# A gated linear attention layer in a two-layer trunk: gate chain beside the input projection, chunk states apart from the products, outputs summed chunk by chunk

## The chip, the core and the metric

One core of one Trainium2 chip runs the whole program. The metric is the device time of one launch in microseconds (us), the median of several runs. The engines are PE (TensorE, matrix products), DVE (VectorE), ACT (ScalarE), POOL (GpSimd) and SP (SyncE, which issues the weight loads). All data is fp32.

## The reference, cut to what matters

There are 512 tokens (256 context, 256 latent) and two layers. Each layer is FFN, token mixing, FFN. The change is in the token mixing of the second layer: a chunked gated linear attention (GLA) with 4 heads (key width 128, value width 256), both directions, chunks of 64 tokens, latent output alone.

```python
logs = [(jax.nn.log_sigmoid((gd @ g_up[d] + g_b[d]).astype(f32)) / GLA_NORMALIZER) for d, gd in ...]
# one direction
b = jnp.cumsum(g, axis=3)                      # within each chunk
scores = einsum(q * jnp.exp(b - b_ref), k * jnp.exp(b_ref - b))
o_intra = einsum(jnp.where(lower, scores, 0.0), v)
q_in = q * jnp.exp(b); k_out = k * jnp.exp(b_last - b); d_last = jnp.exp(b_last[:, :, :, 0])
def step(S, inp):
    o = jnp.einsum('bhck,bhkv->bhcv', qc, S)
    S = S * dc[..., None] + jnp.einsum('bhck,bhcv->bhkv', kc, vc)
    return S, o
# readout
y = o * lax.rsqrt(jnp.mean(jnp.square(o), -1, keepdims=True) + GLA_EPS) * norm_g
return y.reshape(B, T, GLA_DV) * jax.nn.silu(og.astype(jnp.float32))   # then @ w_out
```

## The kernel before

The program is written engine by engine: each engine has its own list of instructions, and semaphores (`S("name")`, `wait_ge`, `then_inc`) tie the lists together. An engine runs its list in order, so a wait holds all that stands behind it. Six sublayers run one after the other; sublayer 4 is the GLA, and its part is `odd_mixer()` in each list, followed by `norm()`.

**Projection.** `OD_TILES` (L2255) lists 33 tiles: 4 of k, one of the low-rank gate input (gd), 4 of q, 16 of v, 8 of the output gate (og). Weights come in pieces of 128x1024. SP loads them into two slots in `arena[:, 0:8192]`, ACT rounds each to `w_hi` (helper `hi`, L642), POOL forms the remainder `w_lo` (L2141), and PE makes three products of every pair. Four pieces are held at a time (columns 8192 to 16384 of the arena). Tile i goes to PSUM bank i mod 8 and ACT copies it out (`z1_done`). The inputs `u_hi` and `u_lo` hold columns 16384 to 24576.

**Gate chain.** Behind the last tile PE makes 8 products of the gate input (32 rows, 512 columns) with `gup`; ACT takes their absolute value, then Exp and Ln over all 4096 columns (L892, L894); DVE takes the minimum with 0 (L2019), subtracts (L2023), sums along the tokens (scan, L2028) and forms the exponents; ACT takes the exponentials (L897 to L906); DVE multiplies them into the keys and queries (L2053 to L2060). The chain's buffers lie where `u_hi` and the weight pieces were.

**Chunks.** PE transposes the keys (L1455, L1461), makes the state products of the context and the scores, then in three rounds the products of the keys and values of one chunk in each direction. In each round DVE adds the old state and multiplies by the decay (L2093, L2096), and the next round waits for that (`gst`). The states `gst` lie in the two weight slots. With all four states there, PE makes the outputs: for each of 8 value tiles, the 128-column product with the masked scores and four 64-column products of states and queries per pair of chunks.

**Readout.** DVE copies the outputs (L2104), ACT squares (L916), PE sums with `ones`, ACT takes Ln and Exp of the sums (L921, L926), DVE multiplies with weight, root and gate (L2113, L2117). ACT and DVE split the result (`out_hi` L734, `out_lo` L1651) and PE starts `project_out`. SP waits for the outputs (`go_mm`) before it loads the output weights; ACT splits their first four pieces behind the Exp.

## Time and profile before

| | us |
|---|---|
| median of 3 runs (2499.55 to 2501.19) | 2499.87 |
| the profiled execution | 2498.56 |
| its span in the profile | 2496.8 |
| projection of the GLA, PE from 1982 to 2083 | 101 |
| from there to the start of `project_out` | 155 |
| PE busy in these 155 us | 84.3 |

### The profile page before, as it was taken

To read this page: it belongs to the slowest core of one execution; us is meant where nothing else is said; L and a number is where in the kernel's file an instruction comes from. 1 tells how busy PE (TensorE), PEld (TensorE's weight loads), DVE (VectorE), ACT (ScalarE), POOL (GpSimd) and SP (SyncE) were. 2 spreads that over 40 slices of the span, in tenths; PEclk is the share of its full clock that TensorE was granted. 3 is DMA by queue.
4 is the path that set the end of the run, shared out by engine and by line. 5 is a ranking of instruction groups with operands and counts; after the bars stand their busy time and mean duration, and the time that the engine had idled before them with its cause. 6 is when DMAs were issued, how large, how long until landed. Compare 5 with 4: busy or idle time off the path is not lost.

```text
span 2496.8 us, 35562 instructions
## 1 busy us (share of the span) xinstructions
PE 2232.4 (89%) x15487; PEld 1800.6 (72%) x15487; DVE 929.5 (37%) x1352; ACT 741.1 (30%) x1065; POOL 937.4 (38%) x429
## 2 busy tenths in 40 slices
PE   5999999799946999978999999899999795578996
PEld 2678877588435888846778777577888594578996
DVE  3322222532487455545330332532131503536213
ACT  2422221533131122135221222522122534126433
POOL 0334434343042121023444334434444352026884
PEclk9999999899977898879999999899999897659998
DMA  9463353230000000022543453263332130023551
GB/s 329 134 227 123 98 193 135 85 134 27 9 0 2 2 3 7 3 101 76 192 171 127 143 203 110 93 212 109 101 101 85 62 121 1 0 101 104 200 170 67
DMA packets 176090, 259.66 MB, mean 104 GB/s; under 512 B 3925, under 2 KB 146275, under 8 KB 175876
## 3 DMA queue, kind: packets, MB, share of 16 engines
q1 hardware_dynamic: 173338, 252.65, 29.9%
q10 hardware_dynamic: 2602, 4.78, 0.5%
q8 instruction: 122, 2.00, 0.3%
q14 instruction: 28, 0.23, 0.0%
HBM read 256.37 MB, written 1.05 MB: 103 GB/s over the span
## 4 chain that ended last, share of the span: by engine, by line
PE 82%; DVE 10%; ACT 5%; issue 1%; DMA 1%; ACTq 0%; SPq 0%; POOL 0%; DVEq 0%; POOLq 0%
PE psum L959 81%; ACT arena L670 1%; ACT u_hi L675 1%; DVE h L1697 1%; DMA arena<-in_ada_w 1%; DVE arena L1854 1%; DVE arena L1865 1%; DMA arena<-in_x 1%; DVE tmp L1710 0%; ACT tmp L720 0%; DVE arena L1831 0%; ACTq L583 0%; DVE arena L2028 0%; PE psum L1301 0%; ACT L730 0%
## 5 line engine op out<-in xcount | busy, mean ns | idle before, releaser
L2141 POOL TENSOR_TENSOR w_lo<-arena,w_hi 128x1024 fp32r<-128x1024 f32 x332 | 811.7, 2450 | 1164.1 <-ACT w_hi L642 1161.8
L959 PE MATMUL psum<-u_hi,w_hi 128*128 128x512 f32 (+1 forms) x1888 | 698.7, 370 | 73.4 <-ACT u_hi L675 39.5
L959 PE MATMUL psum<-u_hi,w_lo 128*128 128x512 f32 (+1 forms) x1888 | 688.1, 365 | 0.0
L959 PE MATMUL psum<-u_lo,w_hi 128*128 128x512 f32 (+1 forms) x1888 | 669.2, 362 | 0.0
L642 ACT ACTIVATE w_hi<-arena 128x1024 fp32r<-128x1024 f32 x332 | 348.4, 1055 | 745.2 <-PE psum L959 733.1
L959 PEld LDWEIGHTS psum<-u_hi,w_hi 128*128 128x128 f32 x1888 | 361.9, 192 | 171.3 <-issue 41.0
L959 PE MATMUL psum<-arena 64*64 64x64 f32 (+8 forms) x5892 | 420.1, 267 | 53.8 <-DVE arena L1887 18.4
L959 PEld LDWEIGHTS psum<-arena 64*64 64x64 f32 (+5 forms) x5892 | 327.4, 158 | 141.0 <-issue 75.3
L959 PEld LDWEIGHTS psum<-u_hi,w_lo 128*128 128x128 f32 x1888 | 362.4, 192 | 54.3
L959 PEld LDWEIGHTS psum<-u_lo,w_hi 128*128 128x128 f32 x1888 | 357.7, 190 | 52.6 <-issue 0.2
L1667 DVE TENSOR_TENSOR tmp<-psum,tmp 128x512 f32<-128x512 f32 (+1 forms) x88 | 54.9, 624 | 592.4 <-ACT tmp L694 592.4
L959 PE MATMUL psum<-hid_hi,w_hi 128*128 128x512 f32 (+1 forms) x704 | 257.4, 366 | 1.7 <-POOL w_lo L2141 1.1
L959 PE MATMUL psum<-hid_hi,w_lo 128*128 128x512 f32 (+1 forms) x704 | 255.3, 363 | 0.0
L959 PE MATMUL psum<-hid_lo,w_hi 128*128 128x512 f32 (+1 forms) x704 | 255.2, 363 | 0.0
L1671 DVE TENSOR_TENSOR hid_lo<-tmp,hid_hi 128x512 f32 (+1 forms) x88 | 200.8, 2282 | 10.8
L959 PEld LDWEIGHTS psum<-hid_hi,w_hi 128*128 128x128 f32 x704 | 132.9, 189 | 24.3 <-DVE mods L1605 1.7
L959 PEld LDWEIGHTS psum<-hid_lo,w_hi 128*128 128x128 f32 x704 | 132.9, 189 | 21.1 <-issue 0.7
L959 PEld LDWEIGHTS psum<-hid_hi,w_lo 128*128 128x128 f32 x704 | 132.9, 189 | 20.8
L694 ACT ACTIVATE tmp<-psum 128x512 f32<-128x512 f32 (+1 forms) x88 | 47.9, 544 | 303.1 <-PE psum L959 303.1
L819 ACT ACTIVATE arena<-psum 128x256 f32<-128x256 f32 x96 | 35.7, 386 | 210.5 <-PE psum L959 208.3
L1681 DVE SCALAR_TENSOR_TENSOR h<-psum,mods,h 128x256 f32<-128x256 f32 x56 | 22.3, 476 | 197.2 <-PE psum L959 197.2
L1697 DVE SCALAR_TENSOR_TENSOR h<-psum,mods,h 128x256 f32<-128x256 f32 x80 | 35.2, 478 | 147.8 <-PE psum L959 147.8
(248 smaller groups left out, 1596.1 us busy)
## 6 DMA issues: line engine op xcount, KB each, us to landing
arena<-in_ada_w SPq DMA_DIRECT2D x48, 1536.0 KB, 6.8
arena<-in_ffn_wg SPq DMA_DIRECT2D x44, 1024.0 KB, 5.3
arena<-in_ffn_wu SPq DMA_DIRECT2D x44, 1024.0 KB, 7.9
arena<-in_ffn_wd SPq DMA_DIRECT2D x20, 2048.0 KB, 8.4
arena<-in_ev_w_in SPq DMA_DIRECT2D x6, 2048.0 KB, 7.7
arena<-in_od_w_in SPq DMA_DIRECT2D x6, 2048.0 KB, 8.4
arena<-in_ffn_wd SPq DMA_DIRECT2D x4, 1024.0 KB, 4.8
arena<-in_ev_w_out SPq DMA_DIRECT2D x2, 2048.0 KB, 10.4
```

The costliest lines, as they stand in the source:

```text
L642: act.activation(piece_shape(split_hi(pc), src), src, ACT.Copy).then_inc(S("hi_done"), 1)
L670: ins = act.activation(us[:, k, s_], hs[:, k, s_], ACT.Identity, scale=modv[:, 24 * (g % 3) + 8 + k, s_:s_ + 1], bias=modv[:, 24 * (g % 3) ...
L675: act.activation(uhv[:, k, T0:NT], uv[:, k, T0:NT], ACT.Copy).then_inc(S("u_hi"), 1)
L694: act.activation(tmp[:, jf * NT:jf * NT + TN], bank[2 * jf][:, 0:TN], ACT.Silu)\
L819: act.activation(blocks(zs[:, d].rearrange("p h t -> p (h t)"), m, d), blocks(bank[d], m, d), ACT.Copy).then_inc(S("zs"), 1)
L959: return pe.matmul(dst, w, x, start=first_, stop=last, skip_group_check=True)
L1667: ve.tensor_tensor(prod, bank[2 * jf + 1][:, 0:TN], prod, ALU.mult).then_inc(S("pairs_free"), 1)
L1671: ve.tensor_tensor(hid_lo[:, at], prod, hid_hi[:, at].bitcast(F32), ALU.subtract)\
L1697: ins = ve.scalar_tensor_tensor(out=hs[:, k, s], in0=bank[b][:, lo:lo + SEG], scalar=modv[:, 24 * (g % 3) + 16 + k, s:s + 1], in1=hs[:, k, s],
L1854: ve.tensor_scalar(dst, tile_of(aa[d], c), col("k_a", c), small[:, 20 + c:21 + c], ALU.mult, ALU.add).then_inc(S("ve_steps"), v.step())
L1865: ve.reciprocal(prep2, prep2).then_inc(S("ve_steps"), v.step())
L2141: pool.tensor_tensor(piece_shape(split_lo(pc), src), src, piece_shape(split_hi(pc).bitcast(F32), src), ALU.subtract).then_inc(S("lo_done"), 1)
```

## The change

It does four things. The 8 gate products become tiles of `OD_TILES` (kind "lg", no weight piece), two behind each q tile; DVE takes the minimum from PSUM, ACT the absolute value, and Exp, Ln and the exponentials run per direction between the copies of tiles (`LG_EXP`, `LG_LN`, `LG_FACTORS` say behind which). DVE forms all keys, queries and decay pairs, then raises `lat_in`. The buffers of the chain move to columns that are free during the projection, and the states to the home of `u_hi` and `u_lo`, so the weight slots stay free: SP loads the output weights without a wait, and POOL and ACT may split them early. The key transposes are one series of 32. The chunk products no longer wait for the states: ACT copies them to SBUF times the decay, and DVE adds old state times decay in one instruction (24 of 256 columns). The outputs are summed in passes: the 128-column products for all 8 tiles, then four passes of 64-column products, one for each state index, into banks 4 to 7. In the readout ACT squares from PSUM, DVE multiplies PSUM with the gate (already times the norm weight), and the Ln table is loaded ahead.

```diff
@@ -350,20 +350,25 @@
...
-        gcs = arena[:, 16384:20480].rearrange("p (d c t) -> p d c t", d=2, c=4)
+        lga = [big[:, 9728:11776], big[:, 11776:13824]]
+        lgb = [arena[:, 24576:26624], arena[:, 41984:44032]]
...
-        gst = arena[:, 0:8192].rearrange("p (d n c v) -> p d n c v", d=2, n=4, c=4)
...
+        gst = arena[:, 16384:24576].rearrange("p (d n c v) -> p d n c v", d=2, n=4, c=4)
...
@@ -563,7 +568,6 @@
...
-                    sp.wait_ge(S("go_mm"), 4)
                     load_cols("odd_out", g, A["od_w_out"][0], [(0, 512), (512, 512)])
...
@@ -875,6 +879,9 @@
...
+                    elif kind == "lg":
+                        act.wait_ge(S("lg_min"), j + 1)
+                        ins = act.activation(gcs[j // 4][:, j % 4], bank[i % 8], ACT.Abs, bias=col("gla_b", j))
...
@@ -883,38 +890,42 @@
...
-                    act.wait_ge(S("lg_psum"), q + 1)
-                    act.activation(gcs[:, d, c], bank[q], ACT.Abs, bias=col("gla_b", q)).then_inc(S("lg_abs"), 1)
...
-                act.activation(arena[:, 16384:20480], arena[:, 16384:20480], ACT.Exp, scale=-1.0).then_inc(S("lg_exp"), 1)
-                act.wait_ge(S("lg_exp"), 1)
-                act.activation(arena[:, 16384:20480], arena[:, 16384:20480], ACT.Ln, bias=eps[:, 3:4]).then_inc(S("lg_ln"), 1)
...
+                    for d, at in enumerate(LG_EXP):
+                        if (kind, j) == at:
+                            act.wait_ge(S("z1_done"), i + 1)
+                            act.activation(lga[d], lga[d], ACT.Exp, scale=-1.0).then_inc(S("lg_exp"), 1)
+                    for d, at in enumerate(LG_LN):
+                        if (kind, j) == at:
+                            act.wait_ge(S("lg_exp"), d + 1)
+                            act.activation(lga[d], lga[d], ACT.Ln, bias=eps[:, 3:4]).then_inc(S("lg_ln"), 1)
+                    for d, at in enumerate(LG_FACTORS):
...
+                            act.wait_ge(S("lat_arg"), d + 1)
+                            act.activation(fl(kout[d]), fl(kout[d]), ACT.Exp, scale=1 / GLA_N)
...
+                            act.activation(fl(qh[d]), fl(kh[d]), ACT.Exp, scale=sign / GLA_N)
+                            act.activation(fl(kh[d]), fl(kh[d]), ACT.Exp, scale=-sign / GLA_N).then_inc(S("lat_exp"), 1)
...
+                for n, q in enumerate(TURNS):
+                    act.wait_ge(S("ko_turned"), n + 1)
+                    dst = kot[n // 2][:, n % 2] if n < 4 else kht[(n - 4) // 2][:, n % 2]
+                    act.activation(dst, bank[q], ACT.Copy).then_inc(S("kot"), 1)
+                for n in range(3):
+                    act.wait_ge(S("gs_mm"), n + 2)
+                    for c in range(4):
+                        for d in range(2):
+                            act.activation(gst[:, d, n + 1, c], bank[4 * (n % 2) + 2 * d + c // 2]
+                                           [:, (c % 2) * HV:(c % 2 + 1) * HV], ACT.Identity,
+                                           scale=gpair[:, d, c, n:n + 1]).then_inc(S("gkv"), 1)
+                for q in range(PIECES):
+                    hi("odd_out", 4, q)
+                act.activation(small[:, 16:17], eps[:, 3:4], ACT.Ln)
...
+                for c in range(4):
+                    act.wait_ge(S("go_mm"), c + 1)
+                    act.activation(sq2[:, 2 * c:2 * c + 2].rearrange("p c t -> p (c t)"), bank[4 + c], ACT.Square)\
...
@@ -1423,10 +1432,17 @@
...
+                    if kind == "lg":
+                        if j == 0:
+                            pe.wait_ge(S("z1_done"), 5)
+                            pe.wait_ge(S("ld_gla"), 48)
+                        mm(bank[i % 8], gup[:, j // 4, (j % 4) * P:(j % 4 + 1) * P], ggd, True, True)\
+                            .then_inc(S("z1_psum"), 1)
+                        continue
...
@@ -1443,69 +1459,65 @@
...
-                pe.wait_ge(S("z1_done"), len(OD_TILES))
-                pe.wait_ge(S("ld_gla"), 48)
-                for q in range(8):
-                    mm(bank[q], gup[:, q // 4, (q % 4) * P:(q % 4 + 1) * P], ggd, True, True)\
-                        .then_inc(S("lg_psum"), 1)
...
+                pe.wait_ge(S("lat_in"), 1)
+                for n, q in enumerate(TURNS):
+                    pe.wait_ge(S("z1_done"), len(OD_TILES) - 7 + n)
...
+                for d in (1, 0):
+                    pe.wait_ge(S("kot"), 8 if d == 0 else 4)
...
-                    pe.wait_ge(S("gst"), n + 1)
...
+                    if n == 0:
+                        pe.wait_ge(S("gst"), 2)
+                    elif n == 1:
+                        pe.wait_ge(S("pm"), 4)
+                    else:
+                        pe.wait_ge(S("gkv"), 8)
+                    for c in range(4):
+                        for d in range(2):
+                            ch = XCHUNK(d, n)
+                            lo = 64 * (ch % 2)
+                            ins = mm(bank[4 * (n % 2) + 2 * d + c // 2][:, (c % 2) * HV:(c % 2 + 1) * HV],
+                                     kht[d][lo:lo + 64, ch // 2, c * P:(c + 1) * P],
                                      gvt[lo:lo + 64, 2 + ch // 2, c * HV:(c + 1) * HV], True, True)
-                    ins.then_inc(S("gs_mm"), 1)
...
+                pe.wait_ge(S("gkv"), 16)
...
+                        mm(out_of(vt_)[:, b * P:(b + 1) * P], gvt[:, 2 + b, vt_ * P:(vt_ + 1) * P],
+                           pm[:, 0, b, vt_ // 2], vt_ % 2 == 0 and b == 0, False)
+                for n in range(4):
+                    for vt_ in range(8):
+                        c = vt_ // 2
+                        if n and vt_ % 2 == 0:
+                            pe.wait_ge(S("gst"), 2 + 8 * (n - 1) + 2 * (c + 1))
+                        for d in range(2):
+                            ch = XCHUNK(d, n)
+                            ins = mm(out_of(vt_)[:, 64 * ch:64 * ch + 64], gst[:, d, n, c, (vt_ % 2) * P:(vt_ % 2 + 1) * P],
+                                     qh[d][:, c, 64 * ch:64 * ch + 64], False, n == 3)
+                        if n == 3 and vt_ % 2:
+                            ins.then_inc(S("go_mm"), 1)
...
@@ -2012,70 +2024,66 @@
...
-                ve.wait_ge(S("z1_done"), len(OD_TILES))
...
+                for i, (q, kind, j) in enumerate(OD_TILES):
+                    if kind == "lg":
+                        ve.wait_ge(S("z1_psum"), i + 1)
+                        ve.tensor_scalar(gg[j // 4][:, j % 4], bank[i % 8], col("gla_b", j), 0.0, ALU.add, ALU.min)\
+                            .then_inc(S("lg_min"), 1)
...
+                    ve.tensor_tensor(lgb[d], lgb[d], lga[d], ALU.subtract).then_inc(S("ve_steps"), v.step())
...
+                        ve.tensor_tensor_scan(gcs[d][:, c], greset, gg[d][:, c], 0.0, ALU.mult, ALU.add)\
...
+                    ve.sem_inc(S("lat_arg"), 1)
+                ve.wait_ge(S("z1_done"), OD_TILES.index((8, "q", 3)) + 1)
...
+                    ve.wait_ge(S("lat_exp"), d + 1)
+                    ve.tensor_tensor(kout[d], kout[d], gk[:, :, 0:SEG], ALU.mult).then_inc(S("ve_steps"), v.step())
+                    ve.tensor_tensor(kh[d], gk[:, :, SEG:NT], kh[d], ALU.mult).then_inc(S("ve_steps"), v.step())
+                    ve.scalar_tensor_tensor(out=qh[d], in0=gq, scalar=HK ** -0.5, in1=qh[d],
...
+                ve.sem_inc(S("lat_in"), 1)
...
@@ -2085,36 +2093,24 @@
...
-                        ve.tensor_tensor(nxt, psum[:, b0 + 2 * d:b0 + 2 * d + 2, :]
-                                               .rearrange("p b (c v) -> p (b c) v", c=2), gst[:, d, n], ALU.add).then_inc(S("ve_steps"), v.step())
-                        ve.wait_ge(S("ve_steps"), v.n)
-                        ins = ve.tensor_tensor(nxt, nxt, gpair[:, d, :, n].unsqueeze(2).to_broadcast([P, 4, HV]),
...
+                    for c in range(4):
+                        ve.wait_ge(S("gst"), 2 if n == 0 else 2 + 8 * (n - 1) + 2 * (c + 1))
+                        for d in range(2):
+                            ve.wait_ge(S("gkv"), 8 * n + 2 * c + d + 1)
+                            ve.scalar_tensor_tensor(out=gst[:, d, n + 1, c], in0=gst[:, d, n, c], scalar=gpair[:, d, c, n:n + 1],
+                                                    in1=gst[:, d, n + 1, c], op0=ALU.mult, op1=ALU.add)\
+                                .then_inc(S("gst"), 1)
...
+                    ve.tensor_tensor(pair_(go), bank[4 + c], pair_(gog), ALU.mult).then_inc(S("ve_steps"), v.step())
...
+                    ve.tensor_tensor(o, o, grs[:, 2 * i:2 * i + 2].unsqueeze(2).to_broadcast([P, 2, 2, SEG]), ALU.mult)\
+                        .then_inc(S("mixed"), 1)
...
@@ -2240,8 +2236,8 @@
...
-                    pool.wait_ge(S("z1_done"), len(OD_TILES))
-                    pool.memset(big[:, 11776:13824], 0.0).then_inc(S("pm_zero"), 1)
+                    pool.wait_ge(S("lat_arg"), 2)
+                    pool.memset(lga[1], 0.0).then_inc(S("pm_zero"), 1)
...
@@ -2252,8 +2248,11 @@
...
-OD_TILES = ([(j, "k", j) for j in range(4)] + [(4, "gd", 0)] + [(5 + j, "q", j) for j in range(4)]
+OD_TILES = ([(j, "k", j) for j in range(4)] + [(4, "gd", 0)]
+            + [at for j in range(4) for at in ((5 + j, "q", j), (None, "lg", 2 * j), (None, "lg", 2 * j + 1))]
             + [(9 + 2 * (j // 4), "v", j) for j in range(16)] + [(17 + j, "og", j) for j in range(8)])
+LG_EXP, LG_LN = (("lg", 3), ("lg", 7)), (("q", 2), ("v", 0))
+LG_FACTORS = (("v", 7), ("v", 15))
```

On PE behind the last projection tile, before: 32 products make the context states and the scores, 24 the chunks, and the outputs go tile by tile. Each row is one run of equal instructions.

```order
L1455 MATMUL psum<-ident,arena 128x128 x16
L1461 MATMUL psum<-ident,arena 128x128 x16
L959 MATMUL psum<-arena 128x256 x16
L959 MATMUL psum<-arena 128x128 x16
L959 MATMUL psum<-arena 128x256 x24
L959 MATMUL psum<-arena 128x128
L959 MATMUL psum<-arena 128x64 x4
L959 MATMUL psum<-arena 128x128
```

The same place after:

```order
L1467 MATMUL psum<-ident,arena 128x128 x32
L968 MATMUL psum<-arena 128x256 x16
L968 MATMUL psum<-arena 128x128 x16
L968 MATMUL psum<-arena 128x256 x24
L968 MATMUL psum<-arena 128x128 x16
L968 MATMUL psum<-arena 128x64 x64
L968 MATMUL psum<-arena,ones 128x256 x8
```

The counts are the same; all 128-column output products now stand ahead of all 64-column ones.

On ACT between the last q tiles and the v tiles of the projection, after (L886 and L888 copy q and v tiles, L884 takes the absolute value, L896 Exp and L900 Ln of one direction):

```order
L884 ACTIVATE arena<-psum,par 128x512 x2
L896 ACTIVATE arena<-arena 128x2048
L646 ACTIVATE w_hi<-arena 128x1024
L886 ACTIVATE arena<-psum 128x256
L900 ACT_TABLE_LOAD
L900 ACTIVATE arena<-arena,eps 128x2048
L884 ACTIVATE arena<-psum,par 128x512 x2
L646 ACTIVATE w_hi<-arena 128x1024
L886 ACTIVATE arena<-psum 128x256
L884 ACTIVATE arena<-psum,par 128x512 x2
L896 ACT_TABLE_LOAD
L896 ACTIVATE arena<-arena 128x2048
```

Before, only `hi` (L642) and the copies (L879, L881) stand here, and this is what stood behind the whole projection:

```order
L890 ACTIVATE arena<-psum,par 128x512 x8
L892 ACT_TABLE_LOAD
L892 ACTIVATE arena<-arena 128x4096
L894 ACT_TABLE_LOAD
L894 ACTIVATE arena<-arena,eps 128x4096
```

Exp and Ln moved in front of the copies of the v tiles and of the splitting of their weights.

## Rows read from the trace of the kernel before

**Rows 1.** The page's chain that ended last, by engine.

```profile
PE 82%; DVE 10%; ACT 5%; issue 1%; DMA 1%; ACTq 0%; SPq 0%; POOL 0%; DVEq 0%; POOLq 0%
```

**Rows 2.** Windows: start:end, length, busy us by engine, PEclk, DMA.

```profile
1982.00:2083.00 101.00, 100.83 (x762) 97.15 (x760) 0.00 (x0) 41.05 (x64) 55.75 (x24) 1.00 0.31 108
2083.00:2238.00 155.00, 84.27 (x337) 70.49 (x337) 71.57 (x76) 40.50 (x47) 12.94 (x5) 0.59 0.08 28
```

**Rows 3.** Timeline of PE: start, us, instruction, idle before and releaser.

```profile
2083.31 11.29 PE L959 MATMUL psum<-arena 32*128 32x512 f32 x16 [0.47 <-ACT arena L884]
2128.97 3.67 PE L1455 MATMUL psum<-ident,arena 128*128 128x128 f32 x16 [34.37 <-DVEq L2055]
2135.24 3.67 PE L1461 MATMUL psum<-ident,arena 128*128 128x128 f32 x16 [2.59 <-DVEq L2062]
2138.71 11.64 PE L959 MATMUL psum<-arena 128*128 128x256 f32 x64
2151.75 2.96 PE L959 MATMUL psum<-arena 64*128 64x256 f32 x16 [1.41 <-DVE arena L2082]
2159.69 5.65 PE L959 MATMUL psum<-arena 64*128 64x256 f32 x16 [4.97 <-DVE arena L2096]
...
2181.05 34.40 PE L959 MATMUL psum<-arena 128*128 128x128 f32 x160 [5.03 <-DVE arena L2096]
2215.24 5.65 PE L959 MATMUL psum<-arena,ones 128*128 128x256 f32 x16
2237.91 0.55 PE L959 MATMUL psum<-u_hi,w_hi 128*128 128x256 f32 x1 [17.02 <-DVE u_lo L1651]
```

**Rows 4.** Windows around the clock's changes, columns as in Rows 2.

```profile
2086.00:2087.00 1.00, 1.00 (x3) 0.48 (x2) 0.86 (x3) 0.70 (x2) 0.00 (x0) 0.55 0.00 0
...
2141.00:2143.00 2.00, 2.00 (x11) 1.76 (x10) 0.00 (x0) 0.00 (x0) 0.00 (x0) 1.00 0.00 0
2147.00:2149.00 2.00, 2.00 (x20) 2.00 (x20) 2.00 (x2) 0.00 (x0) 0.00 (x0) 1.00 0.00 0
...
2185.00:2190.00 5.00, 5.00 (x25) 5.00 (x25) 0.05 (x1) 0.00 (x0) 0.00 (x0) 0.50 0.02 3
...
2242.00:2243.00 1.00, 1.00 (x7) 1.00 (x7) 0.00 (x0) 0.00 (x0) 0.00 (x0) 0.50 1.11 351
```

**Rows 5.** Timeline of ACT, columns as in Rows 3.

```profile
1979.26 1.08 ACT L670 ACTIVATE arena<-h,mods 128x256 f32<-128x256 f32 x2
...
2080.00 0.38 ACT L884 ACTIVATE arena<-psum 128x256 f32<-128x256 f32 x1 [2.50 <-PE psum L959]
...
2121.35 1.91 ACT L897 ACTIVATE arena<-arena 128x2048 f32<-128x2048 f32 x1 [14.78 <-DVEq L2037]
...
2130.37 1.21 ACT L909 ACTIVATE arena<-psum 128x512 f32<-128x512 f32 x2
...
2221.63 1.28 ACT L926 ACT_TABLE_LOAD   x1
2222.92 1.15 ACT L926 ACTIVATE arena<-arena 128x512 f32<-128x512 f32 x2
```

**Rows 6.** Timeline of POOL, columns as in Rows 3.

```profile
2225.09 11.13 POOL L2141 TENSOR_TENSOR w_lo<-arena,w_hi 128x1024 fp32r<-128x1024 f32 x4 [139.97 <-ACT w_hi L642]
```

**Rows 7.** Timeline of DVE, columns as in Rows 3.

```profile
2105.37 4.42 DVE L2023 TENSOR_TENSOR arena<-arena 128x4096 f32<-128x4096 f32 x1 [9.26 <-ACT arena L894]
2109.83 9.03 DVE L2028 TENSOR_TENSOR_SCAN arena<-arena 128x512 f32<-128x512 f32 x8
...
2146.89 2.35 DVE L2074 TENSOR_TENSOR arena<-psum,small 128x1024 f32<-128x1024 f32 x2 [11.07 <-PE psum L959]
...
2234.06 3.24 DVE L2117 TENSOR_TENSOR arena<-arena 128x1024 f32<-128x1024 f32 x1
```

**Rows 8.** Window in the first layer, columns as in Rows 2.

```profile
1069.00:1070.00 1.00, 0.69 (x4) 0.50 (x3) 0.00 (x0) 0.27 (x1) 0.00 (x0) 0.50 0.00 0
```

**Rows 9.** Groups by form in the 4 us before it (1065 to 1069): busy, mean ns.

```profile
L959 PE MATMUL psum<-arena 128*128 128x64 f32 x14 | 2.5, 295 | 0.0
L959 PE MATMUL psum<-arena 64*128 64x64 f32 x16 | 1.8, 296 | 0.0
```

204 lines of the change are left out of this document (66 added, 138 removed).

## The prediction, made before the changed kernel ran

> **What bounds the kernel now.** The page's chain by engine comes first: PE carries 82% of the chain, DVE 10%, ACT 5% [rows 1]. So a change off PE pays only where PE waits for it or runs at the low clock. The windows by stage come next [rows 2]. In the projection PE is busy for 100.83 of 101 us at clock 1.00. In the 155 us behind it PE is busy for 84.27 us, at a mean of 0.59, and no other engine for more than 71.6. This stretch is a chain of engines handing over, and PE's share runs mostly at half speed. The timeline of PE names the pieces [rows 3]: 11.3 us of gate products, 34.4 us of waiting for the gate chain on ACT and DVE, transposes, 11.6 us of state and score products, three rounds of chunk products with 5 us of DVE behind each, 34.4 us of output products, 5.7 us of sums and 17.0 us of waiting for the readout. The change touches all of it and nothing else, so I sum the new path from the end of the projection's products (2083.31 less 0.47 idle: 2082.84) to the first product of project_out (2237.91): 155.1 us before.
>
> **Gate products in the projection.** Before, 8 products took 11.29 us, the first 2.8 us at full clock until it fell at 2086 [rows 3, 4], the rest at half. With p for one at full clock, 2.8/p + 8.4/2p = 8 gives p = 0.87. Eight between the q tiles add 6.9 us to PE, which has no idle time there to hide them. The bound above is 14 (all at half), below 6.8. I take full clock: between pairs of them (1.7 us) stands a dense tile of 2.9 us (0.38 + 2.50 between the copies of two tiles [rows 5]).
>
> **The gate chain behind them.** The wait of 34.4 us and one of 2.6 go [rows 3], if the chain is over before PE's last tile. What is new beside the projection is ACT work: 8 absolute values, two Exp and two Ln of 2048 columns (1.91 each), five table loads of 1.28 [rows 5]. The tight place is the second direction's exponentials behind tile v15: ACT splits two pieces (2.0), copies (0.4), does three exponentials of 1024 columns (half of 1.91 and a little, 3.4 in all), then splits the piece for tile og4 (1.1), and POOL needs 2.4 to 2.8 (11.13 for four [rows 6]). That is 9.3 to 9.7 us, and og4 starts 4 tiles of 2.88, or 11.5 us, behind v15: no stall, with 1.8 us to spare. DVE's part: 4.4 for the subtractions, 9.0 for the scans [rows 7], some 6 for exponents, all while 16 v tiles (46 us) run; then 3.6 us of products per direction. The last are done some 10 us behind v15, 13 us before the projection ends. So lat_in costs nothing; each microsecond beyond those 13 would cost one. The projection ends 6.9 us later and nothing else.
>
> **Transposes and context states**, from that end as zero. Two series of 3.67 us at half clock become one of 32; straight behind dense tiles I take full clock, 3.7 us. ACT's eight copies (0.6 each, 1.21 for two [rows 5]) end near 5; the first state products need four of them, the others eight, at 7.2, so nothing waits. State and score products took 11.64 us, of which 2.2 at half clock until 2141 [rows 3, 4]: 10.5 at full. End: 14.2.
>
> **Chunk products.** A round took 2.96 at full clock and 5.65 at half [rows 3]. The first needs DVE's first states (2.35 [rows 7], done at 13) and runs 14.2 to 17.2; the second runs to 20.2. The third needs ACT's 8 copies of the first: one of 256 columns lies between 0.38 (plain) and 0.54 (two with scale and bias in 1.08) [rows 5]; with scale alone I take 0.45, 3.6 in all, from 17.3 to 20.9. The third ends at 24.0, ACT's second set at 24.5, and with it banks 4 to 7 are free. Heads now alternate between the two halves of the rows, which could shorten a round to no less than 1.5; I keep 3.0, the row's own, as ACT sets two of the three steps. DVE's 24 additions follow ACT and end near 29, before the passes need them. The path from the first round to the last state was 30 us.
>
> **Outputs.** 80 products give 160 records in 34.40 us, 0.215 each at half clock, 0.107 at full (20 in 2.0 us at clock 1.00 [rows 4]); 64 columns cost as much as 128. The 128-column ones: 32 records, 3.4 us, to 28.0. The passes are 128 records. Here the clock decides. For 34 us of such products before it never rose [rows 3, 4], and in the first layer it had fallen to 0.50 [rows 8] behind a stretch made up mostly of 64-column products [rows 9]. I let it fall 4 us into the passes: 37 records at full, 91 at 0.215, 23.6 us in all, to 51.6. Bounds: 13.7 (never falls) and 27.5.
>
> **Readout.** The sums need their 5.65 us [rows 3], the squares beside them: 57.2. Then Ln (0.7), the Exp table (1.28) and the first Exp (0.6) [rows 5]: 60.0 with handovers. Before, the DVE step behind was slowed while POOL split four pieces (3.24 us for 1024 columns [rows 7], 11.13 on POOL [rows 6]). Now the output weights are there early, ACT splits them at 29 to 33 and POOL is done near 42. Two products of 1.2 (half of 2.35 [rows 7]) end at 62.4, and PE starts at 63.0. The copy out of PSUM and a multiplication are gone; the multiplication by the norm weight (1 to 2.5 us on DVE) lies beside the transposes. If POOL were not done, the old 3.24 would return, 4 us in all.
>
> The Trainium skill has a rule on this: ScalarE: Activation LUTs, "Table sets: the hidden batching unit", says one set has both exp and ln, so a change from one to the other needs no load. By it the readout would be 1.3 us shorter. The trace differs: the load of 1.28 stands between Ln and Exp [rows 5], and the sum keeps it.
>
> **Sum.** 6.9 + 63.0 = 69.9 against 155.1: 85.2 us less. The span goes from 2496.8 to 2411.6, the profiled execution from 2498.56 to 2413.4, and the median, which stood 1.3 above it, to 2414.7. Behind the start of project_out nothing changes: PE starts it at half clock, as before.
>
> **Rivals.** (1) The clock holds through the passes. For it: PE no longer pauses for more than a microsecond there. Against: [rows 8, 9]. Passes 13.7 instead of 23.6, sums 3.4 instead of 5.65: 12.1 less, 2402.6. (2) It falls already in the chunk products, which use 64 rows. For it: it fell during products of 32 rows [rows 3, 4]. Against: in 2.96 us of them it held [rows 3]. Second and third round at 5.65 (+4.5, as part hides behind ACT), the 128-column products +3.4, the start of the passes +4.0: 11.9 more, 2426.6. (3) It falls in the transposes: 3.7 us of them stand in one series, and it comes back 2.2 to 5 us into the products (2.2 at 2138.71; at 2242 it was still low, 4 us after 2237.91 [rows 3, 4]). Half of that and up to 1.8 us of the transposes is lost, 1.1 to 4.3: 2417.5. The Trainium skill, TensorE: Matmul & The Clock Gate, "Part 4: PE-mode transpose", says that transposes do not engage the full clock; the trace speaks against it, as the rise 2.2 us behind a series of transposes came sooner than the one without. (4) ACT or POOL late in the projection by more than the 1.8 us: up to 6 us of stalls at og4 to og7, 2418. (5) The chain is not hidden: lat_in comes behind the projection. DVE would have to take more than twice its 20 us; with 5 us over the end, 2420. (6) Slower: the gate products bring the clock down in the projection and it stays at half to its end. The 27 tiles behind them (77.8 us) and the products (6.9) would double, +84.7, and with (2) the time is 2511. It decides from 85 us of such work, so only if it never comes back; the products of project_out, the same as these, brought it back some 5 us after 2237.91 at clock 0.50 [rows 4]. A brief fall costs 2 to 5 us and lies in (4).
>
> **How the numbers follow.** Forecast 0.52, (1) 0.12, (2) 0.15, (3) 0.10, (4) 0.08, (5) 0.02, (6) 0.01. The forecast's own bounds are the moment of the fall (4 us either way), the rounds (2 less) and ACT's copies (1.5 either way). The range from 2401 to 2426 takes these, (1), (3), (4), and half of (2). About 0.2% (5 us) can be told from no change; all but (6) lie far beyond that: faster 0.98, within 0.01, slower 0.01.
>
> **What would show it.** Projection of 108 us at clock 1.00 with no PE idle: the first two parts. PE's first transpose within 0.5 us of the last tile: chain hidden. Third chunk round waiting under 1 us for ACT: the rounds. Granted clock in the 64-column passes: forecast against (1) and (2); clock in the transposes: (3). From the last pass to project_out 11 us against 22.5. A wait for w_lo in the og tiles would be (4).

## The result and the profile of the changed kernel

The changed kernel takes 2395.78 us (median of 4 runs, 2389.39 to 2404.31) against 2499.71 for the kernel before: a ratio of 0.960, 95% interval 0.957 to 0.963. The forecast was 2414.7 with a range from 2401 to 2426, so the kernel is faster than the range allows. Its profiled execution has a span of 2387.6 us, 109.2 less than before.

The chain that ended last, by engine, answers to [rows 1]; PE's share grew from 82% as the waits for DVE and ACT went:

```profile
PE 84%; DVE 8%; ACT 5%; issue 1%; DMA 1%; ACTq 0%; SPq 0%; POOL 0%; DVEq 0%; POOLq 0%
```

Windows of the changed kernel (start:end, length, busy us by engine, PEclk, DMA), to be held against [rows 2]: most of the projection, the stretch behind it up to the first product of project_out, and the first microseconds of that.

```profile
1970.00:2079.00 109.00, 109.00 (x775) 99.89 (x774) 52.09 (x38) 64.61 (x88) 64.32 (x25) 1.00 0.37 126
2080.00:2130.00 50.00, 41.82 (x323) 38.92 (x322) 23.59 (x44) 27.12 (x56) 9.58 (x4) 0.96 0.19 62
2130.00:2135.00 5.00, 5.00 (x32) 5.00 (x32) 1.90 (x6) 1.00 (x2) 0.00 (x0) 0.71 0.00 0
```

PE's timeline of the changed kernel, to be held against [rows 3]. The row at 2083.18 holds the state and score products and two chunk rounds in one piece, that at 2098.90 the last round, that at 2101.92 all output products, and that at 2119.80 the sums.

```profile
1958.15 0.80 PE L968 MATMUL psum<-u_hi,w_hi 128*128 128x512 f32 x1 [6.05 <-ACT u_hi L679]
...
2079.68 3.66 PE L1467 MATMUL psum<-ident,arena 128*128 128x128 f32 x32
...
2083.18 14.30 PE L968 MATMUL psum<-arena 128*128 128x256 f32 x96
2098.90 2.00 PE L968 MATMUL psum<-arena 64*128 64x256 f32 x16 [1.43 <-ACT arena L919]
2101.92 18.05 PE L968 MATMUL psum<-arena 128*128 128x128 f32 x160 [1.02 <-ACT arena L919]
...
2119.80 3.67 PE L968 MATMUL psum<-arena,ones 128*128 128x256 f32 x16
2129.21 0.55 PE L968 MATMUL psum<-u_hi,w_hi 128*128 128x256 f32 x1 [5.74 <-DVE u_lo L1663]
```

Between 2079.68 and 2129.21 lie 49.5 us; before it was 155.1. PE waits 8.2 of them (1.4, 1.0 and 5.7), and the granted clock is 1.00 up to the readout's wait. The same place in the kernel before: the first product of this projection stands at 1969.53, so that the projection took 113.3 us; now it is 121.5.

The other engines, to be held against [rows 5, 6, 7]. First ACT: its copies of the chunk products, its split of the output weights and the table load ahead of the readout's Exp. Then DVE: one of the key products beside the last og tiles, the pair products (the decay pairs), and its last step of the readout. Last POOL, which forms remainders of weights beside those key and pair products.

```profile
2095.82 8.88 ACT L919 ACTIVATE arena<-psum,small 128x256 f32<-128x256 f32 x24 [11.48 <-PE psum L968]
2104.40 4.08 ACT L646 ACTIVATE w_hi<-arena 128x1024 fp32r<-128x1024 f32 x4
...
2124.22 1.28 ACT L937 ACT_TABLE_LOAD   x1
```

```profile
2063.86 3.43 DVE L2066 TENSOR_TENSOR arena<-arena 128x1024 f32<-128x1024 f32 x1
...
2070.56 4.96 DVE L2071 TENSOR_TENSOR small<-small 128x4 f32<-128x4 f32 x6
...
2126.24 2.36 DVE L2112 TENSOR_TENSOR arena<-arena 128x1024 f32<-128x1024 f32 x2 [4.92 <-ACT arena L937]
```

```profile
2063.17 12.10 POOL L2137 TENSOR_TENSOR w_lo<-arena,w_hi 128x1024 fp32r<-128x1024 f32 x4 [0.31 <-ACT w_hi L646]
```

**Where the 109.2 us of the profiled pair came from.** The stretch behind the projection: 155.1 less 49.5, less the 8.2 that the projection grew: 97.3. Behind the start of project_out: 258.9 before (2496.8 less 2237.91), 258.4 now: 0.5. Ahead of the projection, in code that is the same in both: 11.4 (1969.53 less 1958.15). So two questions are left: why this part gave 12 us more than the 85.2 of my sum, and what the 11.4 us are.

### The profile page after: what moved, and what is told of

Its sections match the earlier page's. It is cut to its first block, busy times and chain, and to the rows that moved or that the text cites. A ratio compares the mean times of both kernels' runs of the same rounds, so it can differ in the third digit from the quotient of the medians.

```text
span 2387.6 us, 35611 instructions
## 1 busy us (share of the span) xinstructions
PE 2186.0 (92%) x15487; PEld 1764.1 (74%) x15487; DVE 929.5 (39%) x1354; ACT 750.6 (31%) x1097; POOL 942.9 (39%) x429
## 4 chain that ended last, share of the span: by engine, by line
PE 84%; DVE 8%; ACT 5%; issue 1%; DMA 1%; ACTq 0%; SPq 0%; POOL 0%; DVEq 0%; POOLq 0%
PE psum L968 83%; ACT arena L674 1%; ACT u_hi L679 1%; DVE h L1709 1%; DMA arena<-in_ada_w 1%; DVE arena L1866 1%; DVE arena L1877 1%; DMA arena<-in_x 1%; DVE tmp L1722 0%; ACT tmp L724 0%; ACTq L587 0%; DVE arena L1843 0%; PE psum L1310 0%; ACT L734 0%; DVE arena L2017 0%
## 5 line engine op out<-in xcount | busy, mean ns | idle before, releaser
L968 PE MATMUL psum<-arena 64*64 64x64 f32 (+8 forms) x5892 | 380.1, 258 | 39.4 <-DVE arena L1899 18.4
L968 PEld LDWEIGHTS psum<-arena 64*64 64x64 f32 (+5 forms) x5892 | 294.7, 150 | 117.7 <-issue 70.8
```

The lines of the kernel that those rows point to most:

```text
L968: return pe.matmul(dst, w, x, start=first_, stop=last, skip_group_check=True)
```

## The experiments

A stage time is that from the first transpose (or, where gate products stand ahead of it, from the end of the projection) to the first product of project_out; it is 49.5 in the changed kernel and repeats within 0.1 us. Products of 128 columns are called wide and those of 64 columns narrow; a filler is a product of the identity that nothing uses. The readings rest on the stage times and the timelines. The medians also hold what happens ahead of the stage, which differs by up to 20 us from execution to execution (last section of the experiments). Four kernels ran only once (e5_tiles_warm, e6_wide_last, e7_long_passes, e9_rounds_by_half), so nothing is read from their times.

### Pause and order: the tile order and the wait

The passes undone alone (e1_tiles), and the wait alone that this brings with it (e2_wait):

```diff
 # both
+                pe.wait_ge(S("gst"), 26)
 # e1_tiles alone
                 for vt_ in range(8):
+                    c, dst = vt_ // 2, out_of(vt_)
                     for b in range(2):
...
-                for n in range(4):
-                    for vt_ in range(8):
...
+                        mm(dst[:, b * P:(b + 1) * P], gvt[:, 2 + b, vt_ * P:(vt_ + 1) * P], pm[:, 0, b, c], True, False)
+                        for ch in (2 * b, 2 * b + 1):
+                            for d in range(2):
+                                ins = mm(dst[:, 64 * ch:64 * ch + 64],
+                                         gst[:, d, ch if d == 0 else 3 - ch, c, (vt_ % 2) * P:(vt_ % 2 + 1) * P],
+                                         qh[d][:, c, 64 * ch:64 * ch + 64], False, ch % 2 == 1 and d == 1)
...
```

> The changed kernel with its output products in the order of before: tile by tile, behind a wait for the last state. PE then pauses for some 5.4 us ahead of them (2100.9 to DVE's last addition at 2106.2 in the changed kernel's trace), as before it paused 5 us in each chunk round. Theory A (what decides is whether the clock is up when these products begin, and a pause of 5 us brings it down; they hold a full clock but do not raise it): the granted clock falls at the start of the outputs and stays at half, the 160 records take 34 us instead of 18, and the time is 4.4 + 16 to 19 us above the changed kernel, about 2417. Theory B (the order decides, passes hold the clock and tiles do not): the same numbers here, told apart by the next kernel. Theory C (neither matters, such products always run at full clock once the work ahead of them is dense on average): 18 us at clock 1.00, time 2400 or a little less.

> The changed kernel with one wait more: PE waits for the last state ahead of the 128-column output products, and the passes stay. Theory A (the pause brings the clock down, and the 64-column products do not bring it back): half clock through all outputs, 34 us, time about 2417, like the kernel with tiles. Theory B (the order by passes holds the clock): full clock, outputs 17 to 18 us, time 2400, and only the kernel with tiles is slow. Theory C: 2400 too, and both alike.

PE's timeline of e1_tiles (the output products, then the sums) and windows of it, then PE's output products in e2_wait and windows of that:

```profile
2125.72 34.37 PE L968 MATMUL psum<-arena 128*128 128x128 f32 x160 [5.40 <-DVE arena L2097]
...
2159.88 4.89 PE L968 MATMUL psum<-arena,ones 128*128 128x256 f32 x16
```

```profile
2124.00:2126.00 2.00, 0.28 (x1) 0.31 (x2) 1.57 (x4) 2.00 (x4) 0.87 (x1) 0.70 0.00 0
...
2156.00:2160.00 4.00, 4.00 (x21) 4.00 (x21) 0.00 (x0) 0.00 (x0) 0.00 (x0) 0.50 0.01 4
```

```profile
2116.73 20.88 PE L968 MATMUL psum<-arena 128*128 128x128 f32 x160 [5.41 <-DVE arena L2101]
```

```profile
2116.00:2122.00 6.00, 5.27 (x25) 5.30 (x26) 0.58 (x2) 4.36 (x6) 5.88 (x3) 0.50 0.01 3
2123.00:2124.00 1.00, 1.00 (x12) 1.00 (x11) 0.00 (x0) 0.00 (x0) 1.00 (x2) 1.00 0.00 0
```

Both pause 5.4 us and both start at half clock; the pause brings it down. But in e2_wait it is back 6 us later, while the 32 records of 128 columns run, and the narrow passes behind them run at full clock. In e1_tiles it stays low for all 34 us and comes back only in the sums (4.89 us, where the changed kernel has 3.67). The stages are 71.4 and 56.7 us, which is 21.9 and 7.2 more than in the changed kernel; the medians, 2425.81 and 2409.07 us, lie 30.0 and 13.3 above its 2395.8, so part of that is not the stage's. Theory A is right for the clock of one and wrong for the other (it had 2417 for both), B is wrong on the first step of e2_wait. What differs is where the wide products stand, or the order itself; and whether the tile order also brings a full clock down was not asked.

### Which products hold the clock, and which bring it back

Tile order without the pause (e5_tiles_warm), pause with the wide products behind the passes (e6_wide_last), and ten times the first pass (e7_long_passes):

```diff
 # e5_tiles_warm: e1_tiles with
-                pe.wait_ge(S("gst"), 26)
+                pe.wait_ge(S("gst"), 10)
-                                         gst[:, d, ch if d == 0 else 3 - ch, c, (vt_ % 2) * P:(vt_ % 2 + 1) * P],
+                                         gst[:, d, min(ch if d == 0 else 3 - ch, 1), c, (vt_ % 2) * P:(vt_ % 2 + 1) * P],
 # e6_wide_last: e2_wait with the loop of pm products moved behind the passes
 # e7_long_passes
-                for n in range(4):
+                for n in (0, 0, 0, 0, 0, 0, 0, 0, 0, 0, 1, 2, 3):
```

> Outputs tile by tile as in the kernel e1_tiles, but without the pause ahead of them: the products of the third and fourth chunk states read the second's, which are there (this leaves out the last two states' share of the outputs, not one product). What e1_tiles and e2_wait left open is whether the tile order only fails to bring a fallen clock back, or also brings a full one down. Theory B1 (it holds what it finds; only a pause brings the clock down): 160 records in 17 to 18 us at clock 1.00. Theory B2 (one wide product in five is too little work: the clock falls some microseconds into the tiles even without a pause): 34 us less what runs ahead of the fall, 28 to 31 us, and the pause in e1_tiles was not needed for its loss.

> The kernel e2_wait (a pause of 5.4 us, then the passes) with the 32 records of 128 columns behind the 128 records of 64 columns and not ahead of them. In e2_wait the clock came back 6 us into the outputs, when the wide ones were nearly through. Theory P (the row of wide products brings it back, the narrow ones of the passes would not): the passes run at half clock, 27.5 us, and the clock rises in the wide ones or behind them, 32 to 34 us in all. Theory Q (any unbroken row of products brings it back, and the tile order of e1_tiles failed for another reason): full clock after some 6 us, 20 to 21 us in all as in e2_wait.

> The changed kernel with its first pass done ten times and not once: 416 records of 64 columns behind the wide ones and not 128 (so its output products hold the first chunk's states ten times over). It asks how long such products hold a full clock that they find. In the changed kernel they held it for 13.7 us. Theory H (they hold it as long as PE does not pause): 44.6 us at clock 1.00. Theory F (the clock falls at some point of a long row of them, as it does in the first layer's stretch of such products): the fall shows in the granted clock and the passes take 50 to 85 us; where it falls says how near the changed kernel is to it.

PE's output products in e5_tiles_warm, in e6_wide_last and in e7_long_passes (each row runs over wide and narrow products alike), and windows of the last two:

```profile
2108.12 18.05 PE L968 MATMUL psum<-arena 128*128 128x128 f32 x160 [0.97 <-issue]
```

```profile
2105.88 32.41 PE L968 MATMUL psum<-arena 128*128 128x64 f32 x160 [5.40 <-DVE arena L2102]
```

```profile
2107.00:2133.00 26.00, 26.00 (x124) 26.00 (x123) 0.00 (x0) 2.51 (x4) 7.88 (x4) 0.50 0.26 81
2133.00:2136.00 3.00, 3.00 (x16) 3.00 (x17) 0.11 (x1) 0.60 (x1) 0.00 (x0) 0.52 0.00 0
2136.00:2138.00 2.00, 2.00 (x20) 2.00 (x19) 1.28 (x2) 1.17 (x2) 0.00 (x0) 1.00 0.03 8
```

```profile
2110.29 50.21 PE L968 MATMUL psum<-arena 128*128 128x128 f32 x448 [1.02 <-ACT arena L919]
```

```profile
2114.00:2160.00 46.00, 46.00 (x414) 46.00 (x414) 1.85 (x4) 5.89 (x9) 9.58 (x4) 1.00 0.15 47
```

Without the pause the tile order runs as fast as the passes (18.05 us, the changed kernel's own figure): B1, not B2. In e6_wide_last PE is busy for 26 us without a break at 0.50, and the clock rises only when the wide products run, some 30 us behind the pause: P, not Q. Time alone did not raise it, as in e1_tiles it was still low after 34 us. And the clock stayed full through 46 us of narrow products: H. So for this stage the order by passes gives nothing to the clock by itself. It gives two other things: PE can begin before the last state is there, so the 5.4 us pause is gone, and where a pause does happen, the wide products stand in one piece and bring the clock back.

The Trainium skill, TensorE: Matmul & The Clock Gate, "Why this matters for your kernels", has continuous work as what brings the full clock and idle gaps as what loses it. The traces agree on the gap (0.50 behind 5.4 us in three kernels) and differ on the work: 26 us of unbroken products of 64 columns stayed at 0.50.

### The same with nothing of the change in it

The kernel before with 22 products of the identity ahead of the second and third round and of the outputs:

```diff
+                    for _ in range(22 if n else 0):
+                        mm(bank[4 * ((n + 1) % 2)][:, 0:P], ident[:, :], ident[:, :], True, True)
                     pe.wait_ge(S("gst"), n + 1)
...
+                for _ in range(22):
+                    mm(bank[0][:, 0:P], ident[:, :], ident[:, :], True, True)
                 pe.wait_ge(S("gst"), 4)
```

> The kernel before, with one thing added: while PE waits 5 us for DVE ahead of the second and third chunk round and ahead of the outputs, it runs 22 products of 128 columns of the identity (22 x 0.215 = 4.7 us at full clock) into a bank that is free. Nothing of the change is in it. If pauses bring the clock down, wide products keep it up and narrow ones hold it, the rounds take 2.96 us and not 5.65, the output products in their old tile order 18 and not 34.4, the sums 3.67 and not 5.65: 2.7 + 2.7 + 16.4 + 2.0 = 24 us less than the kernel before. Rival (the tile order itself is slow, or DVE's steps suffer from PE's writes): less than 10 us.

```profile
2151.83 5.18 PE L959 MATMUL psum<-ident 128*128 128x128 f32 x44
2156.94 2.96 PE L959 MATMUL psum<-arena 64*128 64x256 f32 x16
...
2172.93 18.08 PE L959 MATMUL psum<-arena 128*128 128x128 f32 x160
2190.84 4.03 PE L959 MATMUL psum<-arena,ones 128*128 128x256 f32 x16
...
2211.76 0.55 PE L959 MATMUL psum<-u_hi,w_hi 128*128 128x256 f32 x1 [16.89 <-DVE u_lo L1655]
```

The rounds take 2.96 us each, the outputs 18.08 where [rows 3] had 34.40, the stage 131.7 instead of 155.1: 23.3 us less, forecast 24. The ratio to the kernel before is 0.988 (0.985 to 0.992), a median of 2467.38 us. The interval is clear of 1. So some 23 us of what the change gained could be had by fillers in three pauses, without any of its other parts.

### The other parts, one at a time

The gates and their chain behind the projection; the output weights late; a round direction by direction:

```diff
 # e3_gates_behind: the eight "lg" tiles at the end of OD_TILES, and
+LG_EXP, LG_LN = (("lg", 3), ("lg", 7)), (("lg", 7), ("lg", 7))
+LG_FACTORS = (("lg", 7), ("lg", 7))
 # e4_late_weights: hi("odd_out", 4, q) behind the last Exp again, and
+                    sp.wait_ge(S("go_mm"), 4)
                     load_cols("odd_out", g, A["od_w_out"][0], [(0, 512), (512, 512)])
 # e9_rounds_by_half
-                    for c in range(4):
-                        for d in range(2):
+                    for d in range(2):
+                        for c in range(4):
```

> The changed kernel with the first part undone: the eight gate products and the whole chain of exponents stand behind the projection, everything after them as changed. The chain by the durations of the changed kernel's trace: products 6.9, minimum and absolute value 1.5, Exp 1.9, table 1.3, Ln 2.0, DVE 9.6 for one direction and 10.8 for the other, ACT exponentials 3.2, DVE products and pairs 5 to 8: some 43 us from the last tile, 36 more than in the changed kernel. Theory A: the transposes begin at half clock and the clock comes back in the state and score products as it did before (3.7 + 2 to 5 us lost), and from there the rounds and passes follow without a pause and hold it: outputs 18 us at clock 1.00, time about 2396 + 41 = 2437. Rival D (the clock in the passes was held by the dense work of the projection shortly before and not by the products themselves): outputs at half clock, 34 us, time about 2454. If the chain costs less than 30 us more, the sizes in this sum are wrong.

> The changed kernel with the output weights loaded and split late, as before: the load waits for the last output product, ACT splits behind the exponentials. POOL's four pieces then lie beside the readout. My prediction's step: DVE's two products go from 1.2 to up to 3.2 us each and PE's project_out waits 4 us longer, or more if the load itself (2 MB or so) and the splits are late: from the last output product to project_out before took 22.5 us, in the changed kernel it takes 12. Theory A (the late weights are what made the rest of the readout's wait): 5 to 10 us longer, 2401 to 2406. Rival (the load is hidden behind sums and logarithms): within 2 us.

> The changed kernel with the chunk products of a round ordered direction by direction, as before, and not alternating between the two halves of the rows. My sum had 3.0 us for a round, the row of before; the changed kernel's third round took 2.0. If alternating halves are the reason, the third round takes 2.96 us again here and the stage about 3 us more (the third round stands behind ACT's copies, so part of the first two hides). If the length came from something else, the rounds stay at 2.0 us.

PE's timeline of e3_gates_behind, and the window of its output products:

```profile
2119.62 6.44 PE L1467 MATMUL psum<-ident,arena 128*128 128x128 f32 x32 [34.93 <-DVEq L2074]
2125.89 14.30 PE L968 MATMUL psum<-arena 128*128 128x256 f32 x96
```

```profile
2144.00:2162.00 18.00, 17.38 (x156) 17.41 (x156) 6.01 (x15) 10.04 (x19) 9.59 (x4) 1.00 0.16 48
```

From the end of the projection's tiles to project_out 97.9 us, where the changed kernel has 8.2 in the projection and 49.5 behind it: 40.2 more, expected 41; the median is 2435.21, 39.4 more. After a pause of 34.9 us the transposes start at half clock (32 take 6.44 us, in the changed kernel 3.66) and the clock is up before their end, and the narrow products run at full: Theory A of this run, D is out. Hiding the chain is the largest single part of the change.

PE's first product of project_out in e4_late_weights and one behind it, then POOL's four pieces of the output weights, ACT's split of them with the u_hi steps behind it, and DVE's u_lo steps:

```profile
2136.63 0.55 PE L969 MATMUL psum<-u_hi,w_hi 128*128 128x256 f32 x1 [10.65 <-DVE u_lo L1664]
...
2139.03 0.58 PE L969 MATMUL psum<-u_hi,w_hi 128*128 128x256 f32 x1 [1.42 <-DVE u_lo L1664]
```

```profile
2131.55 9.64 POOL L2138 TENSOR_TENSOR w_lo<-arena,w_hi 128x1024 fp32r<-128x1024 f32 x4 [51.80 <-ACT w_hi L647]
```

```profile
2130.41 3.90 ACT L647 ACTIVATE w_hi<-arena 128x1024 fp32r<-128x1024 f32 x4 [1.24 <-DMA arena<-in_od_w_out]
2134.22 2.54 ACT L739 ACTIVATE u_hi<-arena 128x256 fp32r<-128x256 f32 x8
```

```profile
2134.72 8.43 DVE L1664 TENSOR_TENSOR u_lo<-arena,u_hi 128x256 fp32r<-128x256 f32 x8 [3.60 <-ACT u_hi L739]
```

The stage is 54.4 us, 4.9 more: ACT waits 1.24 us for the weights, splits them for 3.9, and only then comes to u_hi, for which DVE waits 3.6. What follows the start of project_out takes 262.6 us instead of 258.4 (2399.2 less 2136.63), 4.2 more, since DVE's u_lo steps are slow beside POOL (8 in 8.43 us; 5 in 1.77 in the changed kernel) and PE waits between its first products. Together that is 9.1, in Theory A's range; the median, 2400.47, lies only 4.7 above the changed kernel's mean of 2395.8, and four executions don't place it closer. My step had only a part of this, and by another row: DVE's two readout products were not slowed here, at 2.36 us for both (POOL starts behind them).

The chunk products of e9_rounds_by_half, grouped by form (busy us, mean ns, idle before):

```profile
L968 PE MATMUL psum<-arena 64*128 64x256 f32 x48 | 8.6, 387 | 0.4 <-ACT arena L919 0.4
```

The 48 records of the three rounds take 8.6 us, so a round is back at 2.9, but the stage is 50.5, 0.9 longer and not 3: the third round's wait for ACT shrinks from 1.4 to 0.4, and the one behind it, 1.0 before the outputs, is gone. The alternating halves are the reason for the 2.0 us, and most of what they save is spent waiting for ACT.

Two parts were not undone alone: the chunk products apart from the states, and the readout's new steps on PSUM. For the readout the rows leave a remainder: PE waited 17.0 us for it before [rows 3], 10.65 with late weights, 5.7 in the changed kernel, so 6.4 of the 11.3 went with these steps and the early table load together. How they share it is not shown.

### The part ahead of the stage

> The changed kernel itself once more. The profiled executions so far began the GLA projection at different times although the code ahead of it is the same: the last fall of the clock ahead of it lies at 1956.6 in the changed kernel, 1967.7 in the kernel before, 1958.8, 1966.4 and 1975.9 in three experiments, and the time at half clock between 790 and 1060 us is 37.5, 54.6, 44.4, 58.0 and 81.9 us. Theory V (the rest of the gain, about 5 us of the median and 10 us in the profiled pair, is the spread of these falls in the first layer, not the change): this run's GLA stage takes again 49.4 us behind the projection and 108 in it, and its start follows its own time at half clock, with half a microsecond for each one. Rival (the change moves something ahead of it): the start of the projection lies near 1957 again, whatever the falls.

The changed kernel once more took 2397.03 us (2388.85 to 2398.21). Its stage is the same to 0.1 us (2088.55 to 2138.07), its projection starts at 1967.04. Windows over the first layer's recurrence in the changed kernel, in this run, in the kernel before and in e1_tiles:

```profile
780.00:1060.00 280.00, 273.17 (x5597) 236.68 (x5595) 148.45 (x312) 60.50 (x155) 42.15 (x36) 0.93 0.01 4
```

```profile
780.00:1060.00 280.00, 273.91 (x5570) 238.57 (x5569) 147.91 (x310) 58.87 (x152) 42.12 (x36) 0.90 0.02 4
```

```profile
780.00:1060.00 280.00, 273.73 (x5585) 239.41 (x5586) 148.20 (x310) 58.17 (x151) 42.12 (x36) 0.89 0.01 4
```

```profile
780.00:1060.00 280.00, 275.07 (x5294) 241.59 (x5294) 140.91 (x294) 55.96 (x145) 42.17 (x36) 0.85 0.01 4
```

Mean clocks of 0.93, 0.90, 0.89 and 0.85 go with starts of the projection at 1958.15, 1967.04, 1969.53 and 1977.56. The mean clock of 280 us alone gives 280 x 0.03 = 8.4 us between the first two, measured 8.9. Eight more profiled executions whose code ahead of the stage is the same fit in: 0.93 goes with 1957.72, 0.92 with 1960.64 and 1960.78, 0.90 with 1964.41, and 0.89 with 1966.52 to 1969.18. This is Theory V: the 11.4 us of the profiled pair are spread of the first layer's clock, and the changed kernel alone shows 8.9 of them. The means say so too. The kernel before, in all its 36 runs, has a mean of 2494.1 us (2482.0 to 2501.2), the changed kernel in its 8 runs 2395.8: 98.3 apart, and the projection, the stage and what follows gave 97.8 in the profiled pair. The runs that the prediction stood on lay at the upper end of that spread.

What makes the clock fall there was asked with fillers in three short waits of every group of the recurrence, wide ones and narrow ones:

```diff
+                        for _ in range(3 if lv == 6 else 0):      # r2: 9 of 64 rows, 64 columns
+                            mm(bank[0][:, 0:P], ident[:, :], ident[:, :], True, True)
...
+                        for _ in range(2 if lv == 5 else 0):      # r2: 6
+                            mm(bank[4][:, 0:P], ident[:, :], ident[:, :], True, True)
...
+                    for _ in range(3 if gi < 7 else 0):           # r2: 9
+                        mm(bank[0][:, 0:P], ident[:, :], ident[:, :], True, True)
```

> The changed kernel, with products of the identity over 128 columns (0.215 us each at full clock) in the three short waits of every group of the first layer's recurrence: 2 ahead of the 32-row products' second step (a wait of 0.32 us), 3 behind them (0.54) and 3 ahead of the next group's turn (0.55). In the traces each fall of the clock between 790 and 1060 us begins some 3.5 us or 11 us behind such a place, in 3 to 6 of the eight groups. Theory S (there the work of PE is too thin to hold the clock, wide products mend it): the falls between 790 and 1060 us are gone or nearly (37 to 82 us at half clock before), which saves about half of them, 19 us and more, less 8 x 0.3 us by which the fillers run over: 2380 or below, and the runs agree better. Rival (the falls come from elsewhere and stand by chance behind these places): as many as before, time 2396 to 2400.

> The same places filled for the same time with products of 64 rows and 64 columns of the identity (6, 9 and 9). Theory S1 (what counts is that PE has no pause): the falls go as in r1_fill_solve. Theory S2 (width counts, narrow products add too little): the falls stay as in the changed kernel, 37 to 82 us between 790 and 1060 us, and the time is 2396 or 2 us more.

Windows of r1_fill_solve ahead of one of its two falls and behind it:

```profile
938.00:950.00 12.00, 12.00 (x205) 10.64 (x203) 6.60 (x13) 3.12 (x8) 0.00 (x0) 1.00 0.00 1
951.00:960.00 9.00, 9.00 (x112) 8.65 (x110) 2.43 (x5) 1.09 (x4) 2.02 (x2) 0.50 0.01 2
```

The time at half clock between 790 and 1060 us is 20.5 us with wide fillers and 41.0 with narrow ones. In both, no fall begins about 3 us behind the 32-row products any more, while two and four begin some 12 us behind them; ahead of the one shown PE was busy for 12.00 of 12 us. The times are 2396.88 and 2403.55 us, so the forecast of 2380 or below was missed: what the wide fillers give back they cost, as in every other group only the first of the three waits is there and the fillers lengthen the place by some 2 us. So these waits go with part of the falls, and a filler of either width mended that part, as far as one profiled execution of each shows. The falls some 12 us behind came with no pause of PE ahead of them, and their cause stays open.

Last, wide fillers in all the waits of the six norms and in the readout:

> The changed kernel with products of the identity (128 columns, 0.215 us at full clock) where PE waits: 24 in the readout of the GLA stage (5.74 us of waiting), and in each of the six layer norms 24 ahead of the means (5.5 us; 12 and 19 in the last two) and 26 behind them (6.05 to 6.7 us; 22 and 35 in the last two), into a bank whose sum DVE has read. By the reading of the clock so far (pauses of 3 to 6 us bring it down, wide products keep it up) project_out of the GLA stage starts at full clock (2.6 us less), and the half-clock stretches at the norms (13.7 us at 478, 6.8 at 1161, 13.7 at 1560, 13.7 at 1957, 6.8 at 2137, 13.7 at 2168 in the changed kernel) go: about half of the part of each in which PE works, 3 to 4 us a norm, some 20 us in all, 2376. Rival (the products delay the real ones by what they run over, or slow ACT and DVE in the norms): within 5 us of the changed kernel.

```profile
2126.46 5.52 PE L968 MATMUL psum<-ident 128*128 128x128 f32 x48
2132.35 0.36 PE L968 MATMUL psum<-u_hi,w_hi 128*128 128x256 f32 x1 [0.38 <-DVE u_lo L1670]
```

The clock does stay up: its mean over the program is 0.970 and not 0.955, and project_out starts at full clock; what follows its start takes 254.7 us, not 258.4. But the time is 2393.64 us (ratio 0.9598, 0.9574 to 0.9621), which can't be told from the changed kernel's 0.9601. At the head of a stage PE takes each piece of u as ACT delivers it, with 0.45 us of waiting per piece even at full clock: the first four pieces of the projection take 6.6 us in both kernels, at half clock and at full. So there the half clock cost nearly nothing. The 20 us were wrong. The rival has the size right and not the reason: it had the fillers delaying the real products or slowing ACT and DVE.

## Why the prediction was wrong, step by step

- **Gate products**: 6.9 us at full clock, measured 8.2, at clock 1.00 with no idle time, so rivals (4) and (6) are out. Right in kind, 1.3 short.
- **The chain is hidden**: right, and e3_gates_behind shows it. The first transpose follows the last tile at once. But DVE was done at 2075.5 (the pair products end it), 4 us ahead and not 13: two of its three products behind the second exponentials took 3.4 us each beside POOL where I had 1.2 (the first 1.8), and the six pair products, for which I had nothing, 5.0. In the kernel before, with POOL idle, the same steps took 1.2 and, all six together, 0.55:

```profile
2132.77 1.22 DVE L2058 SCALAR_TENSOR_TENSOR arena<-arena 128x1024 f32<-128x1024 f32 x1
...
2135.27 0.55 DVE L2067 TENSOR_TENSOR small<-small 128x4 f32<-128x4 f32 x6
```

Rival (5), a chain over the end, was nearer than its 0.02.

- **Transposes, states and scores**: 3.7 and 10.5, right, at full clock; rival (3) is out. The Trainium skill's rule that transposes do not engage the full clock (TensorE: Matmul & The Clock Gate, "Part 4: PE-mode transpose") has no support here: in e3_gates_behind the clock came back some 5.5 us into a series of 32 transposes, with nothing else on PE since a pause of 34.9 us.
- **Chunk rounds**: 3.0 each was the row of before, measured 2.0 with alternating halves, at clock 1.00 (rival (2) is out). ACT's copies 0.37, taken 0.45. The outputs start at 22.2 behind the zero and not at 24.5: 2.3 us.
- **Outputs, the step that failed**: I let the clock fall 4 us into the passes, 27.0 us in all; it held, and they took 17.9 us, 9.1 less. [Rows 3, 4] show that narrow products had not raised a clock that a pause of 5 us had brought down; I read from them that they bring it down. [Rows 8, 9] show a fall behind such work, but also behind still thinner products and short waits. Rival (1), with 0.12, was what happened; e1_tiles, e5_tiles_warm, e6_wide_last and e7_long_passes show the mechanism, the pause that the change took away.
- **Sums**: 5.65 was the row at half clock, measured 3.67: 2.0 us, by the same cause.
- **Readout**: 5.8 from the sums to project_out, measured 5.7. Right. The table load between Ln and Exp is still there with its 1.28 us, as the sum had kept it.
- **Nothing changes behind the start of project_out**: 0.5 us. Right.

Together 9.1 + 2.0 + 2.3 less 1.3 is 12.1, which is 97.3 less 85.2. With the clock alone right the forecast would have been 2403.6 (2414.7 less 11.1), with every term right 2401.9 (2499.7 less 97.8), both within the old range. The range was narrow on that side: rival (1) at 2402.6 together with rounds 2 us shorter, a bound that the forecast itself gave, lies below 2401. The rest to 2395.8 is the first layer's spread, for which the range had nothing. The runs of before that the prediction had, within 1.6 us of each other (2499.55 to 2501.19), had looked like a kernel without spread; from the mean of all 36, 2494.1, the same 97.8 us lead to 2396.3.

## What to carry to other kernels

A stretch at half clock has two causes to look for apart: what brought the clock down (here pauses of 5 us) and what doesn't bring it back (here rows of 64-column products on 128 rows). Before costing such products at the clock of the old trace, ask which of the two the change removes; and test it with a few wide products in the pause, which in the old kernel alone gave 23 us. But fill only where PE sets the pace behind the pause: fillers in the norms raised the mean clock from 0.955 to 0.970 and gave next to nothing.

## What the runs showed of the hardware

- Products of 64 columns on 128 rows, back to back for 26 us, left the granted clock at 0.50; within 3 us of 128-column products behind them it was 1.00 (e6_wide_last). The same products ran for 46 us at a clock of 1.00 that they had found (e7_long_passes).
- A pause of PE of 5.4 us was followed by half clock each time (e1_tiles, e2_wait, e6_wide_last); waits of 1.0 and 1.4 us in the chunk rounds were not.
- Rounds of 64-row products took 2.0 us where successive products alternate between the two halves of the rows, and 2.9 where four in a row use the same half (e9_rounds_by_half).
- Beside POOL's work on weights a DVE multiplication of 128x1024 took 3.4 us and six of 128x4 took 5.0 together; with POOL idle they took 1.2 and 0.55.
- In the first layer's recurrence the clock falls at other groups from run to run (mean 0.85 to 0.93 over 280 us), which moves the whole time by up to 20 us (start of the projection at 1957.72 to 1977.56). One fall, in r1_fill_solve, came with PE busy for the 12 us ahead of it.
